# Two column chunks of a feed-forward tile computed side by side in two PSUM banks, in a two-block transformer kernel on one core

## Chip, cores and metric

The kernel runs on one core of a Trainium2 chip. The metric is the device time of one execution in microseconds (us). Before the change the median of three runs is 4473.61 us (4471.12 to 4476.59).

## What is computed

Two blocks in sequence work on 1024 tokens of width 1024 (and, in the first block, 256 context tokens). Each has two layers. The change touches only the feed forward of the second block, which runs once per layer:

```
def conv_ffn(h, w_up, conv_w, conv_b, w_down):
    up = h @ w_up                                  # 1024 -> 2 * 2816
    padded = jnp.pad(up, ((0, 0), (2, 0), (0, 0)))
    conv = conv_b + padded[:, 0:s_len] * conv_w[0]
    for j in range(1, 3):
        conv = conv + padded[:, j:j + s_len] * conv_w[j]
    gate, val = jnp.split(conv, 2, axis=-1)
    return (jax.nn.silu(gate) * val) @ w_down      # 2816 -> 1024
```

Everything is float32. The kernel gets that precision from three matmuls in a rounded format for each product: a value is split into a rounded part (hi) and the rest (lo), and w_hi\*hi + w_hi\*lo + w_lo\*hi is summed.

## The kernel before, in words

**Layout.** Activations lie with channels on the 128 partitions and the 1024 tokens along the free dimension. A weight tile is 128 output channels; it is an entry of the list SEQ with its number g, its count nk of 128-row contraction steps, and its column chunks. In the feed forward every tile has two chunks of 512 tokens (CH_LAT). The 2816 hidden channels are 22 pairs f of up tiles, tile 2f (gate) and tile 2f+1 (value), with nk = 8. The down projection is done in six groups of hidden channels, (0,4), (4,8), (8,12), (12,16), (16,19), (19,22), each with eight output tiles d of nk = 4 or 3. A group's down tiles stand behind the up tiles of f = 4, 8, 12, 16, 19 and 21 (the dictionary AFTER), so that a group's last activation has one f of time to be made.

**Chunks and banks.** All chunks of the program are numbered q in order, and chunk q is accumulated in PSUM bank q % 3 (psum_of). So a chunk can start when chunk q-3 has been taken out of its bank: PE (TensorE) waits for `acc_free{q % 3}` to reach q // 3, and when the last matmul of a chunk has finished it raises `acc_ready`.

**PE, lines 498 to 514 (project).** A tile waits for its split weights (`w_split`), then chunk after chunk: wait for the bank, then for each of the nk rows the three matmuls of lines 511, 512 and 513. A tile of nk = 8 has 2 x 24 matmuls of 512 columns. Lines 471 to 495 (row_tile, project_as_ready) take both chunks of a row in turn, three matmuls in each bank, because the rows become ready one at a time; the first up tile of a layer is done so. The feed forward's order on PE is lines 916 to 928.

**ACT (ScalarE), lines 1308 to 1322.** For each f in order: the four up chunks are copied out of PSUM (line 1178, in evacuate2), each as soon as it is ready; then ACT waits for the convolution of f on DVE (`ff_conv`) and applies Silu (line 1320), waits for the product (`ff_prod`) and writes g_hi (line 1322). Only then does it turn to the chunks of f+1:

```
for f in range(NF):
    n = NF * l + f
    up(f)
    act.wait_ge(sem["ff_conv"], n + 1)
    A(ff_c[0], ff_c[0], ACT.Silu).then_inc(sem["ff_gated"], 1)
    act.wait_ge(sem["ff_prod"], n + 1)
    A(g_hi[:, f % NG], ff_c[1], ACT.Copy).then_inc(sem["ff_hi"], 1)
```

**DVE (VectorE), lines 1745 to 1782.** For each f: it waits until all four chunks are copied (`ff_up_ready`), computes the convolution of the gate and the value tile (lines 1765, 1767, 1769, twice), waits for Silu, multiplies (1775), waits for g_hi, writes g_lo (1779) and raises `g_ready`. Where down tiles follow on PE, it adds their 16 chunks to the residual (line 1757) and frees their banks, one chunk between every two of those steps, the rest afterwards; for f = 21 all adds come at the end.

**POOL (GpSimd), lines 1795 to 1804.** Splits the weights of tile g into w_hi (1802) and w_lo (1803), once all chunks of tile g-2 are ready. SP (SyncE) loads the weights, two tiles ahead.

Of the kernel before, what the change touches and what calls it, by code (L numbers as in the profile page):

```python
# [19 lines left out]
P = 128  # L20
# [21 lines left out]
NG = 5  # L42
# [9 lines left out]
def stream():  # L52

    seq = []
    for l in range(2):
        for i, n in enumerate(IN1):
            seq.append(("in1", l, i, 8, CH_ALL if l == 0 or n in KV1 else CH_LAT))
        for d in range(DT):
            seq.append(("out1", l, d, 8, CH_ALL if l == 0 else CH_LAT))
    for l in range(2):  # L60
        for i, n in enumerate(IN2):
            seq.append(("in2", l, i, 8, CH_LAT))
        for d in range(DT):
            seq.append(("out2", l, d, 8, CH_LAT))
        for f in range(NF):
            seq.append(("up", l, 2 * f, 8, CH_LAT))
            seq.append(("up", l, 2 * f + 1, 8, CH_LAT))
            if f in AFTER:
                g = AFTER[f]
                for d in range(DT):  # L70
                    seq.append(("down", l, (g, d), GROUPS[g][1] - GROUPS[g][0], CH_LAT))
    return seq


SEQ = stream()
INDEX = {e[:3]: g for g, e in enumerate(SEQ)}
FIRST_CHUNK = np.cumsum([0] + [len(e[4]) for e in SEQ]).tolist()
# [66 lines left out]
def two_mixers(nc, xT, cT, w_mod, w_in1, w_out1, vec1, vec2, vec3, sinks, gla_up,  # L144
# [5 lines left out]
    def put(name, floats, dt=F32, where=None):  # L150
        offset = at[0] if where is None else where
        place[name] = offset
        if where is None:
            at[0] += (floats + -floats % 8) * 4
        assert offset + floats * 4 <= 229368, name
        return nc.alloc_sbuf_tensor_at(name, [P, floats], dt, offset=offset)

    raw = put("raw", 2 * 1024)
    w_hi = put("w_hi", 2 * 1024, F32R)
    w_lo = put("w_lo", 2 * 1024, F32R)  # L160
# [23 lines left out]
    h2_hi = h2_hi_[:, :].rearrange("p (j t) -> p j t", t=S)  # L184
    h2_lo = h2_lo_[:, :].rearrange("p (j t) -> p j t", t=S)
# [18 lines left out]
    def k(name):  # L204
        c, n = CONST_AT[name]
        if name in ("dec", "qdec", "kdec"):
            c -= NC1
            return cst2[:, c:c + n]
        if c > NC1:
            c -= 2048  # L210
        return cst[:, c:c + n]


    a = Area(wk1, 0, n1)
# [4 lines left out]
    a = Area(wk1, 0, n1)  # L219
# [5 lines left out]
    a = Area(wk1, 0, n1)  # L225
# [9 lines left out]
    a = Area(wk1, 0, n1)  # L235
# [7 lines left out]
    a = Area(gw, 0, 2 * DT * T)  # L243
# [16 lines left out]
    a = Area(wk2, 0, n2)  # L260
# [3 lines left out]
    a = Area(wk2, 0, n2)  # L264
# [9 lines left out]
    a = Area(wk2, 0, n2)  # L274
# [8 lines left out]
    g_hi = put("g_hi", NG * S, F32R, where=work2)[:, :].rearrange("p (f t) -> p f t", t=S)  # L283
    g_lo = put("g_lo", NG * S, F32R, where=work2 + NG * S * 4)[:, :].rearrange("p (f t) -> p f t", t=S)
    a = Area(wk2, 2 * NG * S, n2)
# [24 lines left out]
    sem = {n: nc.alloc_semaphore(n) for n in names}  # L310
# [40 lines left out]
    def psum_of(q):  # L351
        return psum[q % 3]


    with block:
# [111 lines left out]
        def _(pe):  # L467
            mm = nc.tensor.matmul
# [22 lines left out]
            def project_as_ready(g, hi, lo, ready, before):  # L491

                for kt in range(SEQ[g][3]):
                    row_tile(g, kt, hi, lo, ready, before)

            def project(g, hi, lo, f0=None, only=None):

                _, _, _, nk, chunks = SEQ[g]
                pe.wait_ge(sem["w_split"], g + 1)
                wh, wl = w_hi[:, (g % 2) * 1024:], w_lo[:, (g % 2) * 1024:]  # L500
                for ci, (t0, n) in enumerate(chunks):
                    if only is not None and ci != only:
                        continue
                    q = FIRST_CHUNK[g] + ci
                    if q >= 3:
                        pe.wait_ge(sem[f"acc_free{q % 3}"], q // 3)
                    o = psum_of(q)[:, 0:n]
                    for kt in range(nk):
                        ws = slice(kt * P, (kt + 1) * P)
                        at_ = kt if f0 is None else (f0 + kt) % NG  # L510
                        mm(o, wh[:, ws], hi[:, at_, t0:t0 + n], start=kt == 0, stop=False)  # L511
                        mm(o, wh[:, ws], lo[:, at_, t0:t0 + n], start=False, stop=False)  # L512
                        last = mm(o, wl[:, ws], hi[:, at_, t0:t0 + n], start=False, stop=kt == nk - 1)  # L513
                    last.then_inc(sem["acc_ready"], 1)

            def modulate(row, w):

                for kt in range(DT):
                    last = mm(row, csil[:, 2 * kt:2 * kt + 2], w[:, :, kt * P:(kt + 1) * P], start=kt == 0, stop=kt == DT - 1)
                last.then_inc(sem["wm_used"], 1)  # L520
# [9 lines left out]
            def add_square(n, j, chunks, sq):  # L530

                pe.wait_ge(sem["sq_ready"], 8 * n + j + 1)
                for ci, (t0, w) in enumerate(chunks):
                    last = mm(psum[3 + ci][:, 0:w], k("ones"), sq[j % 2][:, t0:t0 + w], start=j == 0, stop=j == 7)  # L534
                last.then_inc(sem["sq_used"], 1)
# [7 lines left out]
            for u in range(4):  # L543
                pe.wait_ge(sem[f"wm_in{u}"], 16)
                modulate(START_BANKS[u][0:2, :], gw[:, u * 4096:(u + 1) * 4096].rearrange("p (m c) -> p m c", c=D))
                if u:
                    turn_modulation(u - 1, 4, mod_row[:, (u - 1) * 512:u * 512], 4 * (u - 1))
            turn_modulation(3, 4, mod_row[:, 1536:2048], 12)
            for l in layers:
# [4 lines left out]
                chunks = CH_OUT[l]  # L554
                c0 = chunk_count(l)
                if l == 0:
# [9 lines left out]
                    a = len(LATE_MOD)  # L566
                    turn_modulation(3 + a, 2, mod_row[:, (a - 1) % 2 * 256:], 2 * (a - 1))
                project(proj_index(l, "bk"), h_hi, h_lo)
                for j in range(2):
                    pe.wait_ge(sem["conv_ready"], 2 * l + j + 1)  # L570
                    for ci, (t0, w) in enumerate(chunks):
                        last = mm(psum[3 + ci][:, 0:w], k("ones256"), cv_a[j][:, t0:t0 + w], start=j == 0, stop=j == 1)
                last.then_inc(sem["mean_ready"], 1)
                for j in range(2):
                    pe.wait_ge(sem["csq_ready"], 2 * l + j + 1)
                    for ci, (t0, w) in enumerate(chunks):
                        last = mm(psum[3 + ci][:, 0:w], k("ones256"), cv_sq[:, t0:t0 + w], start=j == 0, stop=j == 1)
# [16 lines left out]
                for t in range(NTT):  # L594
                    last = nc.tensor.transpose(psum[3 + t // 4][:, (t % 4) * P:(t % 4 + 1) * P], at_raw[:, t * P:(t + 1) * P], ident)
# [68 lines left out]
                for t in range(NTT):  # L664
                    mm(psum[3 + t // 2][:, (t % 2) * 256:(t % 2 + 1) * 256], gl_lr[:, t * P:(t + 1) * P], gl_up,
                       start=True, stop=True).then_inc(sem["z_ready"], 1)
# [90 lines left out]
                for n, t in enumerate(BORD):  # L757
                    gt = NTT * l + n
                    pe.wait_ge(sem["sb_ready"], gt + 1)
                    if outs or t < NBLK:  # L760
                        if n >= 2:
                            pe.wait_ge(sem["obb_added"], outputs(l, n) - 2)
                        for c in (1, 0):
                            for j in range(2):
                                last = mm(psum[5 + n % 2][:, j * P + c * 64:j * P + (c + 1) * 64],
                                          gl_s[(2 * n + 1 - c) % 6][:, j * P:(j + 1) * P],
                                          gl_qd[:, 1, t * P + c * 64:t * P + (c + 1) * 64],
                                          start=(c, j) == (1, 0), stop=c == 0, skip_group_check=True)
# [4 lines left out]
                for j in range(2):  # L773
                    for ci, (t0, w) in enumerate(chunks):
                        b, o = [(3, 0), (4, 0), (5, 0)][ci] if j == 0 else [(6, 0), (7, 0), (5, 256)][ci]
                        last = mm(psum[b][:, o:o + w], k("ones64"), gl_sq[:, j * T + t0:j * T + t0 + w], start=True, stop=True)
# [10 lines left out]
            for l in layers:  # L787
# [6 lines left out]
                for t in range(NBLK):  # L794
                    for j in range(2):
                        o = (t % 2) * 256 + j * P
                        last = nc.tensor.transpose(psum[3 + t // 2][:, o:o + P], sg_v[j][:, t * P:(t + 1) * P], ident)
# [3 lines left out]
                for j in range(2):  # L801
                    for n in range(NBLK):
                        for h in (2 * j, 2 * j + 1):
                            last = mm(psum[3 + 2 * j + n // 4][:, (n % 4) * P:(n % 4 + 1) * P], sg_vz[:, n, h, :],
                                      sg_ws[:, h * P:(h + 1) * P], start=h % 2 == 0, stop=h % 2 == 1)
# [3 lines left out]
                for j in range(2):  # L809
# [5 lines left out]
                    for ci in range(2):  # L815
                        last = mm(psum[3 + ci][:, :], po_w[:, j * P:(j + 1) * P], po_p[j][:, ci * 512:(ci + 1) * 512], start=True, stop=True)
# [55 lines left out]
                for j in range(4):  # L872
# [19 lines left out]
                    for t in range(NBLK):  # L892
                        last = mm(psum[5 + t // 4][:, (t % 4) * P:(t % 4 + 1) * P], re_kd[:, t * P:(t + 1) * P],
                                  re_v[:, t * P:(t + 1) * P], start=True, stop=True)
# [21 lines left out]
                for f in range(NF):  # L916
                    if f == 0:
                        project_as_ready(INDEX[("up", l, 0)], h2_hi, h2_lo, "h_ready", nh)
                    else:
                        project(INDEX[("up", l, 2 * f)], h2_hi, h2_lo)  # L920
                    project(INDEX[("up", l, 2 * f + 1)], h2_hi, h2_lo)
                    if f in AFTER:
                        g = AFTER[f]
                        f0, f1 = GROUPS[g]
                        pe.wait_ge(sem["g_ready"], NF * l + f1)
                        for d in range(DT):
                            project(INDEX[("down", l, (g, d))], g_hi, g_lo, f0)
                            if f == NF - 1 and d:
                                add_square(5 + 2 * l, d - 1, CH_LAT, f_sq)
                add_square(5 + 2 * l, DT - 1, CH_LAT, f_sq)  # L930
# [1057 lines left out]
```

## Time and profile before

| | |
|---|---|
| median of three runs | 4473.61 us |
| span of the profiled execution, first to last instruction | 4469.6 us |
| PE busy | 4037.1 us, 90% |
| DVE, ACT, POOL busy | 43%, 24%, 25% |
| mean granted TensorE clock | 0.960 of full speed |
| matmuls of lines 511 to 513, all parts | 12552 |
| feed forward, layer 0 and layer 1 of the second block | about 2386 to 3150 us and 3680 to 4450 us |

The profiled execution has no time of its own beside its span; the span lies 4.0 us below the median of the runs, which is what lies around it and the spread between runs. Busy shares are averages over parts with different limits. Matmuls overlap in the pipeline: a row's duration (0.39 us) is longer than the distance to the next start (0.23 us), so a rate is read from starts. "Idle before" is the time in which the engine had nothing in flight, and the releaser is what ended it.

### The profile page before, as it was taken

To read this page: it belongs to the slowest core of one execution; us is meant where nothing else is said; L and a number is where in the kernel's file an instruction comes from. 1 tells how busy PE (TensorE), PEld (TensorE's weight loads), DVE (VectorE), ACT (ScalarE), POOL (GpSimd) and SP (SyncE) were. 2 spreads that over 40 slices of the span, in tenths; PEclk is the share of its full clock that TensorE was granted. 3 is DMA by queue.
4 is the path that set the end of the run, shared out by engine and by line. 5 is a ranking of instruction groups with operands and counts; after the bars stand their busy time and mean duration, and the time that the engine had idled before them with its cause. 6 is when DMAs were issued, how large, how long until landed. Compare 5 with 4: busy or idle time off the path is not lost.

```text
span 4469.6 us, 46828 instructions
## 1 busy us (share of the span) xinstructions
PE 4037.1 (90%) x18692; PEld 3153.4 (71%) x18692; DVE 1938.5 (43%) x2630; ACT 1066.3 (24%) x1934; POOL 1105.8 (25%) x764
## 2 busy tenths in 40 slices
PE   6979999798399998899989999998999799999997
PEld 3657778686277776578766888886677567888885
DVE  2655651815656445332324454444333325444543
ACT  3014542202145421312312111111222312111112
POOL 0021002222110121133312333333233123333331
PEclk9989999999699998999989999999999899999998
DMA  4310000022000001211111111111210021111111
GB/s 158 133 61 20 10 12 15 27 69 84 10 20 10 21 5 52 94 48 34 38 48 47 48 43 43 50 46 39 89 38 34 24 71 36 52 50 48 48 48 52
DMA packets 60857, 209.22 MB, mean 47 GB/s; under 512 B 6752, under 2 KB 11872, under 8 KB 59488
## 3 DMA queue, kind: packets, MB, share of 16 engines
q1 hardware_dynamic: 60640, 206.22, 13.5%
q8 instruction: 149, 2.44, 0.2%
q14 instruction: 68, 0.56, 0.0%
HBM read 189.42 MB, written 16.78 MB: 46 GB/s over the span
## 4 chain that ended last, share of the span: by engine, by line
PE 78%; DVE 16%; ACT 3%; issue 2%; DMA 1%; POOL 0%; SPq 0%; DVEq 0%; ACTq 0%; POOLq 0%
PE bank L511 21%; PE bank L512 20%; PE bank L513 20%; DVE wk L1414 4%; PE bank L534 2%; PE bank L630 2%; DVE wk L1359 2%; PE bank L616 1%; DVE h_lo L1348 1%; DVE gw L1538 1%; DVE gw L1549 1%; PE bank L607 1%; PE bank L605 1%; DVE wk L1471 1%; PE bank L485 1%
## 5 line engine op out<-in xcount | busy, mean ns | idle before, releaser
L511 PE MATMUL bank<-h_hi,w_hi 128*128 128x512 f32 (+1 forms) x3480 | 1370.3, 394 | 16.8 <-POOLq L1804 9.3
L512 PE MATMUL bank<-h_lo,w_hi 128*128 128x512 f32 (+1 forms) x3480 | 1344.6, 386 | 0.0
L513 PE MATMUL bank<-h_hi,w_lo 128*128 128x512 f32 (+1 forms) x3480 | 1344.4, 386 | 0.0
L1802 POOL CAST w_hi<-raw 128x1024 fp32r<-128x1024 f32 (+2 forms) x306 | 302.7, 989 | 2565.2 <-PE bank L513 1954.5
L511 PEld LDWEIGHTS bank<-h_hi,w_hi 128*128 128x128 f32 x3480 | 657.3, 189 | 173.3 <-issue 17.6
L512 PEld LDWEIGHTS bank<-h_lo,w_hi 128*128 128x128 f32 x3480 | 657.1, 189 | 152.4 <-issue 12.2
L513 PEld LDWEIGHTS bank<-h_hi,w_lo 128*128 128x128 f32 x3480 | 656.5, 189 | 143.2
L1803 POOL TENSOR_TENSOR w_lo<-raw,w_hi 128x1024 fp32r<-128x1024 f32 (+2 forms) x306 | 638.3, 2086 | 24.5
L511 PE MATMUL bank<-g_hi,w_hi 128*128 128x512 f32 x704 | 284.5, 404 | 26.6 <-DVEq L1780 26.6
L1765 DVE TENSOR_SCALAR wk<-wk,v 128x1024 f32<-128x1024 f32 x88 | 86.7, 986 | 478.3 <-ACTq L1314 475.5
L1178 ACT ACTIVATE wk<-bank 128x512 f32<-128x512 f32 x192 | 114.4, 596 | 742.8 <-PE bank L513 733.1
L512 PE MATMUL bank<-g_lo,w_hi 128*128 128x512 f32 x704 | 279.3, 397 | 0.0
L513 PE MATMUL bank<-g_hi,w_lo 128*128 128x512 f32 x704 | 279.1, 396 | 0.0
L1757 DVE TENSOR_TENSOR x<-bank,x 128x512 f32<-128x512 f32 x192 | 132.8, 692 | 243.1 <-PE bank L513 238.5
L485 PE MATMUL bank<-h_hi,w_hi 128*128 128x512 f32 x176 | 86.8, 493 | 133.6 <-DVE h_lo L1348 71.6
L1414 DVE SCALAR_TENSOR_TENSOR wk<-wk,v 128x1024 f32<-128x1024 f32 (+1 forms) x180 | 191.1, 1090 | 4.3
L1767 DVE SCALAR_TENSOR_TENSOR wk<-wk,v 128x1024 f32<-128x1024 f32 x88 | 186.2, 2116 | 5.3
L511 PEld LDWEIGHTS bank<-g_hi,w_hi 128*128 128x128 f32 x704 | 133.3, 189 | 61.6 <-DVEq L1780 27.5
L630 PE MATMUL bank<-wk 128*128 128x128 f32 x1280 | 166.5, 276 | 0.0
L1320 ACT ACTIVATE wk<-wk 128x1024 f32<-128x1024 f32 x44 | 46.7, 1061 | 465.3 <-DVEq L1772 465.3
L512 PEld LDWEIGHTS bank<-g_lo,w_hi 128*128 128x128 f32 x704 | 133.3, 189 | 33.9 <-issue 2.9
L485 PEld LDWEIGHTS bank<-h_hi,w_hi 128*128 128x128 f32 x176 | 40.5, 230 | 163.9 <-issue 64.8
(247 smaller groups left out, 4714.9 us busy)
## 6 DMA issues: line engine op xcount, KB each, us to landing
raw<-w_in SPq DMA_DIRECT2D x90, 512.0 KB, 3.5
raw<-w_ffn SPq DMA_DIRECT2D x88, 512.0 KB, 3.5
x<-w_mod SPq DMA_DIRECT2D x16, 1024.0 KB, 4.8
raw<-w_out SPq DMA_DIRECT2D x32, 512.0 KB, 4.4
raw<-w_down SPq DMA_DIRECT2D x64, 256.0 KB, 2.6
residual<-x SPq DMA_DIRECT2D x3, 4096.0 KB, 12.0
wk<-residual SPq DMA_DIRECT2D x24, 512.0 KB, 3.5
gw<-w_mod SPq DMA_DIRECT2D x4, 2048.0 KB, 23.4
```

Of the source, the lines that this page charges most:

```text
L485: mm(o, wh[:, ws], hi[:, kt, t0:t0 + n], start=kt == 0, stop=False)
L511: mm(o, wh[:, ws], hi[:, at_, t0:t0 + n], start=kt == 0, stop=False)
L512: mm(o, wh[:, ws], lo[:, at_, t0:t0 + n], start=False, stop=False)
L513: last = mm(o, wl[:, ws], hi[:, at_, t0:t0 + n], start=False, stop=kt == nk - 1)
L534: last = mm(psum[3 + ci][:, 0:w], k("ones"), sq[j % 2][:, t0:t0 + w], start=j == 0, stop=j == 7)
L630: last = mm(out_bank(i)[:, 0:P], at_vz[:, kt, g, :], at_pt[i % 2][:, c * P:(c + 1) * P], start=g == 0 and c == 0, stop=g == 1 and c == len ...
L1178: link(A(dst[:, t0:t0 + w], psum_of(q)[:, 0:w], func, scale=scale))
L1414: ins = V.scalar_tensor_tensor(dst, src, vl("conv_w", 31 * j + i), dst, ALU.mult, ALU.add)
L1757: link(V.tensor_tensor(x2[:, d, t0:t0 + w], psum_of(q)[:, 0:w], x2[:, d, t0:t0 + w], ALU.add))
L1767: link(V.scalar_tensor_tensor(c, u[:, 1:S + 1], w2("conv_w", 44 + wi), c, ALU.mult, ALU.add))
L1802: link(G.tensor_copy(w_hi[:, sl], raw[:, sl]))
L1803: link(G.tensor_tensor(w_lo[:, sl], raw[:, sl], w_hi[:, sl].bitcast(F32), ALU.subtract))
```

## The change

In the feed forward, project is replaced by project_side_by_side for every tile but the first up tile of a layer. The new function works in nk + 2 steps. In a step it takes row `step` of chunk 0 and row `step - 2` of chunk 1, and each of the three terms is issued for chunk 0 and then for chunk 1, so that consecutive matmuls go to two banks in turn. In the first two steps there is only chunk 0, in the last two only chunk 1. PE waits for the bank of chunk 0 at the tile's start and for that of chunk 1 before the third step.

```
@@ -512,6 +512,30 @@
+            def project_side_by_side(g, hi, lo, f0=None):
+
+                _, _, _, nk, chunks = SEQ[g]
+                pe.wait_ge(sem["w_split"], g + 1)
+                wh, wl = w_hi[:, (g % 2) * 1024:], w_lo[:, (g % 2) * 1024:]
+                (t0, n), (t1, _) = chunks
+                q0, q1 = FIRST_CHUNK[g], FIRST_CHUNK[g] + 1
+                o0, o1 = psum_of(q0)[:, 0:n], psum_of(q1)[:, 0:n]
+                pe.wait_ge(sem[f"acc_free{q0 % 3}"], q0 // 3)
+                lead = 2
+                for step in range(nk + lead):
+                    k0, k1 = step, step - lead
+                    if k1 == 0:
+                        pe.wait_ge(sem[f"acc_free{q1 % 3}"], q1 // 3)
+                    for term in range(3):
+                        w, v = (wl if term == 2 else wh), (lo if term == 1 else hi)
+                        for kt, o, t, q in ((k0, o0, t0, q0), (k1, o1, t1, q1)):
+                            if 0 <= kt < nk:
+                                a = kt if f0 is None else (f0 + kt) % NG
+                                last = mm(o, w[:, kt * P:(kt + 1) * P], v[:, a, t:t + n], start=kt == 0 and term == 0,
+                                          stop=kt == nk - 1 and term == 2)
+                                if kt == nk - 1 and term == 2:
+                                    last.then_inc(sem["acc_ready"], 1)
@@ -917,14 +941,14 @@
                     if f == 0:
                         project_as_ready(INDEX[("up", l, 0)], h2_hi, h2_lo, "h_ready", nh)
                     else:
-                        project(INDEX[("up", l, 2 * f)], h2_hi, h2_lo)
-                    project(INDEX[("up", l, 2 * f + 1)], h2_hi, h2_lo)
+                        project_side_by_side(INDEX[("up", l, 2 * f)], h2_hi, h2_lo)
+                    project_side_by_side(INDEX[("up", l, 2 * f + 1)], h2_hi, h2_lo)
...
                         for d in range(DT):
-                            project(INDEX[("down", l, (g, d))], g_hi, g_lo, f0)
+                            project_side_by_side(INDEX[("down", l, (g, d))], g_hi, g_lo, f0)
```

## Rows read from the trace of the kernel before

**Rows 1.** The page: the clock line, and the chain that ended last by engine.
```profile
PEclk9989999999699998999989999999999899999998
...
PE 78%; DVE 16%; ACT 3%; issue 2%; DMA 1%; POOL 0%; SPq 0%; DVEq 0%; ACTq 0%; POOLq 0%
```
**Rows 2.** A group by line, page: count, busy, mean ns, idle before, releaser.
```profile
L511 PE MATMUL bank<-g_hi,w_hi 128*128 128x512 f32 x704 | 284.5, 404 | 26.6 <-DVEq L1780 26.6
```
**Rows 3.** Busy time by stretch: us, PE, PEld, DVE, ACT, POOL, PEclk, DMA, GB/s.
```profile
2416.00:3020.00 604.00, 604.00 (x2590) 485.84 (x2589) 289.72 (x216) 84.84 (x115) 205.70 (x141) 1.00 0.14 46
3700.00:4340.00 640.00, 640.00 (x2756) 518.86 (x2755) 310.24 (x237) 88.75 (x119) 220.32 (x155) 1.00 0.15 47
```
**Rows 4.** Timeline of ACT, one f: start, duration, line [idle before <-releaser].
```profile
2616.55 0.60 ACT L1178 ACTIVATE wk<-bank 128x512 f32<-128x512 f32 x1 [5.00 <-PE bank L513]
...
2628.89 1.06 ACT L1322 ACTIVATE g_hi<-wk 128x1024 fp32r<-128x1024 f32 x1 [1.35 <-DVEq L1776]
2629.86 1.29 ACT L1178 ACTIVATE wk<-bank 128x512 f32<-128x512 f32 x2
2633.35 0.60 ACT L1178 ACTIVATE wk<-bank 128x512 f32<-128x512 f32 x1 [2.20 <-PE bank L513]
```
**Rows 5.** Timeline of PE: chunk ends (L513) and starts (L511) within one f.
```profile
2616.12 0.39 PE L513 MATMUL bank<-h_hi,w_lo 128*128 128x512 f32 x1
2616.35 0.40 PE L511 MATMUL bank<-h_hi,w_hi 128*128 128x512 f32 x1
...
2627.55 0.40 PE L511 MATMUL bank<-h_hi,w_hi 128*128 128x512 f32 x1
...
2632.92 0.39 PE L513 MATMUL bank<-h_hi,w_lo 128*128 128x512 f32 x1
2633.15 0.40 PE L511 MATMUL bank<-h_hi,w_hi 128*128 128x512 f32 x1
```
**Rows 6.** Timeline: a matmul that waited for a bank, earlier in the program.
```profile
105.67 0.60 ACT L998 ACTIVATE wk<-bank 128x512 f32<-128x512 f32 x1
106.45 0.47 PE L511 MATMUL bank<-h_hi,w_hi 128*128 128x512 f32 x1 [1.10 <-ACTq L999]
106.76 0.39 PE L512 MATMUL bank<-h_lo,w_hi 128*128 128x512 f32 x1
```
**Rows 7.** Timeline of DVE beside down tiles of nk = 4.
```profile
2644.62 0.69 DVE L1757 TENSOR_TENSOR x<-bank,x 128x512 f32<-128x512 f32 x1 [0.67 <-PE bank L513]
2645.45 2.26 DVE L1769 SCALAR_TENSOR_TENSOR wk<-wk,v 128x1024 f32<-128x1024 f32 x1
```
**Rows 8.** Timeline of PE: one row of a tile taken in two banks.
```profile
1041.35 0.39 PE L486 MATMUL bank<-h_lo,w_hi 128*128 128x512 f32 x1
1041.58 0.40 PE L487 MATMUL bank<-h_hi,w_lo 128*128 128x512 f32 x1
1041.81 0.40 PE L485 MATMUL bank<-h_hi,w_hi 128*128 128x512 f32 x1
1042.06 0.40 PE L486 MATMUL bank<-h_lo,w_hi 128*128 128x512 f32 x1
```
**Rows 9.** Timeline of PE: 256 columns; then 512 columns at a lower clock.
```profile
308.08 0.28 PE L511 MATMUL bank<-h_hi,w_hi 128*128 128x256 f32 x1
308.20 0.28 PE L512 MATMUL bank<-h_lo,w_hi 128*128 128x256 f32 x1
...
2387.42 0.63 PE L485 MATMUL bank<-h_hi,w_hi 128*128 128x512 f32 x1
2387.85 0.63 PE L486 MATMUL bank<-h_lo,w_hi 128*128 128x512 f32 x1
```
**Rows 10.** Busy time by stretch, columns as above, around short idle times of PE.
```profile
1040.50:1054.50 14.00, 8.54 (x32) 5.76 (x33) 12.17 (x22) 5.91 (x9) 0.07 (x1) 1.00 0.00 0
...
312.00:316.00 4.00, 2.38 (x6) 1.93 (x7) 0.00 (x0) 1.51 (x6) 1.63 (x1) 0.64 0.31 70
...
2386.50:2391.00 4.50, 4.50 (x12) 3.41 (x11) 4.43 (x5) 2.11 (x2) 0.00 (x0) 0.50 0.00 0
```

## The prediction

> **What bounds the kernel now.** I read the page first. TensorE is granted the full clock nearly everywhere, and the chain that ended last is 78% PE [rows 1]; in the feed forward it is PE alone, so I looked there for anything that PE waits for. The groups by line show no wait on a bank: the 704 first matmuls of the down tiles have 26.6 us of idle time, all for g_lo of the last f (13.3 us per layer) [rows 2]. The busy time by stretch then says that PE has no idle time at all over 604 and 640 us [rows 3]. The reader should see two things there: the stage's time is the number of matmuls times their distance, and 604/2590 is 0.2332 us, 640/2756 is 0.2322 us. So the change can act in two ways only: on that distance, or by making PE wait where it now does not.
>
> The second needs the order on ACT. ACT copies the last chunk of an f at 2616.55, then waits for DVE twice, ends g_hi at 2628.89 + 1.06 = 2629.95, and only then takes the first chunk of the next f out of its bank, two chunks in one row from 2629.86 [rows 4]. That chunk had been complete since about 2622, 5.6 us after the f began. It hurts nobody now: the bank is wanted by the fourth chunk, and that starts at 2633.15 [rows 5].
>
> **The change, part by part.** I call the four chunks of an up pair a0 to a3.
>
> *Matmuls, loads, semaphores.* The number of matmuls, of weight loads and of signals stays the same; a0 of a tile is ready after 41 of 48 matmuls instead of after 24, a1 at the tile's end as before. POOL's split waits for whole tiles, so its start, SP's loads and the collisions of POOL with DVE stay where they are relative to the tile's end. No term.
>
> *The wait for the bank of a3.* Bank q % 3 makes a3 wait for a0. Before, a3 starts 24 matmuls into the second tile. Now PE asks for its bank after 6 matmuls, in front of the third step, and all that PE has left of the tile is queued behind that wait. The second tile starts at 2627.55 [rows 5]; 6 matmuls of 0.2333 later is 2628.95. The copy of a0 starts at 2629.86 and takes 0.60 like the single ones [rows 4], so it ends at 2630.46. Where PE has waited for such a copy, its matmul started 0.18 us after the copy's end (105.67 + 0.60 = 106.27, start 106.45), and the next came 0.31 later instead of 0.23 [rows 6]. PE resumes at 2630.64: 1.69 us of wait, 0.08 for the slower start, 1.77 in all. ACT's chain hangs on the end of the previous f and not on a0, so nothing in this change shortens it.
>
> *How often.* It happens where the f before has no down tiles behind it: with them, DVE and ACT are through with that f long before a0 is ready. Of f = 0 to 21, f = 0 and those behind 4, 8, 12, 16 and 19 are free of it, which leaves 16 per layer, 32 in all. In layer 1 the same reading shifts by a few hundredths, since the matmuls are 0.2322 apart; I don't carry that. 32 x 1.77 = **+56.6 us**. Bounds: 32 x 1.4 = 45 if the copy were handed over at once and the last matmuls before the wait overlapped it, 32 x 2.1 = 67 if the hand-over cost twice what it does in rows 6.
>
> *The other banks.* a1 wants the bank that held a2 of the f before. Now a2 is complete 7 matmuls before its tile's end and a1 begins 6 matmuls into the next: 13 x 0.233 = 3.0 us for a copy of 0.60 plus hand-over. ACT waits for exactly that copy then. Nothing. The down tiles have the same 3.0 us for their first chunk, where they had two chunks, 5.6 or 4.2 us; their cover is DVE, whose add takes 0.69 but can stand behind a step of up to 2.26 us [rows 7]. The last matmul ends and hands over in some 0.4 us (started 2632.92, copied from 2633.35 [rows 4, 5]), so 0.43 + 0.69 + 0.18 = 1.3 leaves about 2.0 us for DVE. Setting DVE's steps against the new completion times (4.0, 5.6, 9.6, 11.2 us and so on for nk = 4, 2.6, 4.2, 6.8, 8.4 for nk = 3) I find the adds in time; in the worst phase one is late by 0.3 us, and 12 groups x 4 such adds x 0.3 = 14 us is the upper bound. I take 0. At f = 21 all adds come afterwards, one per chunk, and have room.
>
> *The distance between matmuls.* The tiles done side by side are 86 of nk = 8, 64 of nk = 4 and 32 of nk = 3. In the two first and two last steps one chunk runs alone (12 matmuls), so 36, 12 and 6 matmuls of a tile alternate: 3096 + 768 + 192 = 4056 of 6240. Does a change of bank help? In a tile taken row by row at full clock the distances are 0.23 in one bank, 0.23 over the change of bank (1041.58 to 1041.81) and 0.25 behind it [rows 8]; the change from a3 to the next a0 is 0.23 too, 2616.12 to 2616.35 [rows 5]. And what a matmul takes beyond one column per cycle goes with its columns: 256 columns are 0.12 apart, half of 0.233, while at half clock 512 columns are 0.43 apart, 512 cycles of 1.2 GHz and nothing more [rows 9, 10]. A cost of reopening the same bank would be a constant per matmul. I take **0**. Bounds: the best is one column per cycle at 2.4 GHz, 0.2133 us, 20 ns less; the worst is 0.01 more, half of what rows 8 show behind a change.
>
> What 20 ns would bring is less than 4056 x 20 = 81 us. In each of the 32 waiting f the gain of the first tile (36 x 20 ns = 0.72 us) only makes PE arrive earlier at the same wait: 32 x 0.72 = 23 us are swallowed, 58 us remain. The worst side is 4056 x 0.01 = 41 us, less what the wait swallows, 29.
>
> The Trainium skill (TensorE: Matmul & The Clock Gate, Back-to-back issue gap) gives a warm matmul of N columns as N / 2.4 plus 2.5 ns, 215.8 ns for 512. The trace differs: 0.2322 to 0.2333 us. By that rule as the goal of the alternation the sum would be about 4473.6 + 57 - 2904 x 17 ns = 4481 us.
>
> **Sum.** 4469.6 + 56.6 = 4526.2 us of span for the profiled execution; the median of the runs is 4.0 above that span, so **4530 us**, 1.3% slower. About 0.2% (9 us) is what a measurement of this kernel can tell from no change.
>
> **The rivals.**
>
> *A. The alternation brings the matmuls down to a column per cycle.* Against it: rows 5, 8 and 9. For it: one change of bank in 24 or in 3 matmuls is not a change at every one. 4530 - 58 = 4472 us, no difference. Chance 0.06. The two parts would then cancel.
>
> *B. Matmuls into different banks overlap, and the kernel is faster.* The place is the same, the 2904 alternating matmuls (4056 less 32 x 36) that are not swallowed. It decides from 66 / 2904 = 23 ns of gain on, a distance below 0.2107 us, which is under the column per cycle; so two matmuls would have to stream at once. If the bank were all the limit, the distance could halve: 2904 x 0.1167 = 339 us, 4191 us. Nothing in the rows speaks for it; the half clock's 0.43 is just the columns. Chance 0.03.
>
> *C. The new waits make the clock fall.* PE is idle for some 1.5 us every 24 us. For it: around idle times of that length the clock was 0.64 in one stretch; against it: it stayed 1.00 over four waits of 1.64 us in 14 us, with PE busy in 8.54 of them [rows 10], and here PE is busy before and behind. If it fell each time for six matmuls (at 312 to 316), 6 x 0.2 = 1.2 us, 32 x 1.2 = 38 us: 4568 us. Chance 0.08. The same page of the Trainium skill (A second HAM failure mode) says that cycling through PSUM banks lets PE idle briefly between groups, so that the clock goes up and down; by it C would be likelier than I make it. The trace before cycles through three banks and shows 1.00 in both stretches [rows 3].
>
> *D. The bank's waits are as forecast, and DVE's adds or a slower change of bank come on top.* 4530 + 14 + 29 = 4573 at the most, 4545 in the middle. Chance 0.11.
>
> *E. The wait is covered after all,* because the copy of a0 comes earlier than I read it. The order on ACT is written out and nothing moves it, so only if my reading of which bank is wrong: 4474 us. Chance 0.02.
>
> **How the numbers follow.** The forecast has 0.70, within 4518 to 4542 by the bounds of the wait. With D up to 4552 and a part of a smaller gain on the other side I come to the range 4512 to 4556, about 8 in 10; C's top and A, B, E stay outside. Faster by over 0.2%: B, 0.03. Within 0.2%: A (where its gain is nearly whole) and E, 0.06. Slower: the rest, 0.91.
>
> **What the changed profile would show.** Idle time of PE with the copy of line 1178 on ACT as releaser, 32 times, about 1.5 us each and 50 us in all (the rest is drain and slower start), none for f behind down tiles; the distance from one f to the next in such a pair 24.2 us instead of 22.4; the distance between alternating matmuls 0.232 to 0.233; DVE's adds without PE waiting for them; the clock 1.00 in both stretches. I am wrong if the distance falls below 0.23, if the waits are fewer or for another engine, or if the clock drops behind them.

## The result, and the profile after

| | before | after |
|---|---|---|
| median of the runs | 4475.07 us (4471.12 to 4476.59, 4 runs) | 4529.37 us (4527.12 to 4530.09, 4 runs) |
| span of the profiled execution | 4469.6 us | 4525.3 us |
| ratio to before | | 1.0123, 95% interval 1.0109 to 1.0138 |

The median before counts one run more than the one given ahead of the prediction (4473.61 us). The changed kernel is 1.2% slower, 54 us by the medians and 55.7 us by the spans; the prediction was 4530 us.

The page of the changed kernel has these lines against [rows 1, 2]. Line 535 is the one matmul line of the new function; ACT's copy of an up chunk, line 1178 before, is now line 1202, and ACT's signal for a free bank is line 1203.

```profile
PEclk9989999899699999999999999999999899999998
PE 68%; DVE 23%; ACT 5%; issue 2%; DMA 1%; POOL 0%; DVEq 0%; SPq 0%; ACTq 0%; POOLq 0%
L535 PE MATMUL bank<-h_hi,w_hi 128*128 128x512 f32 x1376 | 463.0, 397 | 46.5 <-ACTq L1203 46.5
...
L535 PE MATMUL bank<-g_hi,w_hi 128*128 128x512 f32 x704 | 258.0, 403 | 26.6 <-DVEq L1804 26.6
```

The clock line is as before but for a digit in three slices, and the mean is 0.959 of full speed where it was 0.960. In the chain that ended last PE has 68% where it had 78%; DVE has 23% where it had 16%, and ACT 5% where it had 3%. In the up tiles there are 46.5 us of idle time that did not exist, all for one releaser; the down tiles have what they had, 26.6 us for g_lo of the last f, and nothing for DVE's adds. (All matmuls of the new function have line 535, so the page tells them apart by their operands. Where two consecutive ones have the same operands, a timeline prints one row, "x2", whose time runs from the start of the first to the end of the second.)

The waits view of the changed kernel: engine, line and what it waited for, total us, times, longest.

```profile
PE bank L535 <- ACTq L1203: 46.5, 32, 1.5
```

32 waits, as counted in the prediction. The stretch of busy time that answers to the first of [rows 3]:

```profile
2416.00:3020.00 604.00, 583.64 (x2495) 468.50 (x2494) 275.51 (x208) 80.76 (x109) 204.34 (x136) 1.00 0.15 45
```

PE was busy for all of the 604 us before and misses 20.4 us now, with 95 matmuls fewer in the same time; the clock is 1.00 in both. In the second stretch of [rows 3] the changed kernel has 30.1 us of idle time and a clock of 0.99. The low clock there lies before 3714 us, where the feed forward of that layer has not yet come to its first wait (3750.62):

```profile
3700.00:3714.00 14.00, 6.70 (x17) 4.94 (x17) 9.97 (x9) 7.83 (x9) 0.00 (x0) 0.63 0.13 39
3714.00:4340.00 626.00, 603.20 (x2574) 482.96 (x2573) 285.20 (x220) 86.74 (x116) 207.35 (x138) 1.00 0.15 44
```

One wait, in the timeline of ACT (start, duration, line, idle time before):

```profile
2602.99 0.60 ACT L1202 ACTIVATE wk<-bank 128x512 f32<-128x512 f32 x1 [1.03 <-PE bank L535]
2612.93 1.06 ACT L1344 ACTIVATE wk<-wk 128x1024 f32<-128x1024 f32 x1 [9.33 <-DVEq L1796]
2615.34 1.06 ACT L1346 ACTIVATE g_hi<-wk 128x1024 fp32r<-128x1024 f32 x1 [1.35 <-DVEq L1800]
2616.30 1.30 ACT L1202 ACTIVATE wk<-bank 128x512 f32<-128x512 f32 x2
2625.44 0.60 ACT L1202 ACTIVATE wk<-bank 128x512 f32<-128x512 f32 x1 [7.84 <-PE bank L535]
2627.07 0.60 ACT L1202 ACTIVATE wk<-bank 128x512 f32<-128x512 f32 x1 [1.03 <-PE bank L535]
```

and in that of PE:

```profile
2614.87 0.39 PE L535 MATMUL bank<-h_lo,w_hi 128*128 128x512 f32 x1
2615.10 0.40 PE L535 MATMUL bank<-h_hi,w_lo 128*128 128x512 f32 x1
2616.97 0.72 PE L535 MATMUL bank<-h_hi,w_hi 128*128 128x512 f32 x2 [1.48 <-ACTq L1203]
2617.53 0.63 PE L535 MATMUL bank<-h_lo,w_hi 128*128 128x512 f32 x2
2618.00 0.63 PE L535 MATMUL bank<-h_hi,w_lo 128*128 128x512 f32 x2
```

ACT's chain from the last chunk of an f to the copy of the next f's first chunk is what it was: 2602.99 to 2616.30 is 13.31 us, and 2616.55 to 2629.86 was 13.31 us [rows 4]. PE has issued 6 matmuls of the second tile, would issue the next at 2615.33, and starts at 2616.97: 1.64 us late. The first pair then takes 0.56 us instead of 0.47. Together 1.73 us. This is one of the longer waits: its idle time is 1.48 us, and the mean of the 32 is 46.5 / 32 = 1.45. From one f's last copy to the next it is 2627.07 - 2602.99 = 24.08 us, against 22.40 before in this layer (96 matmuls of 0.2333 us).

### The profile page after: what moved, and what is told of

It is laid out like the page before. It is cut to its first block, busy times and chain, and to the rows that moved or that the text cites. A ratio compares the mean times of both kernels' runs of the same rounds, so it can differ in the third digit from the quotient of the medians.

```text
span 4525.3 us, 46828 instructions
## 1 busy us (share of the span) xinstructions
PE 4046.4 (89%) x18692; PEld 3154.1 (70%) x18692; DVE 1931.1 (43%) x2630; ACT 1066.1 (24%) x1934; POOL 1115.9 (25%) x764
## 4 chain that ended last, share of the span: by engine, by line
PE 68%; DVE 23%; ACT 5%; issue 2%; DMA 1%; POOL 0%; DVEq 0%; SPq 0%; ACTq 0%; POOLq 0%
PE bank L535 23%; PE bank L511 10%; PE bank L513 9%; PE bank L512 9%; DVE wk L1438 4%; DVE wk L1791 3%; PE bank L558 2%; PE bank L654 2%; DVE wk L1793 2%; DVE wk L1383 2%; DVE wk L1789 1%; PE bank L640 1%; DVE h_lo L1372 1%; DVE gw L1573 1%; DVE wk L1799 1%
## 5 line engine op out<-in xcount | busy, mean ns | idle before, releaser
L511 PE MATMUL bank<-h_hi,w_hi 128*128 128x512 f32 (+1 forms) x2104 | 827.2, 393 | 16.7 <-POOLq L1828 9.1
L512 PE MATMUL bank<-h_lo,w_hi 128*128 128x512 f32 (+1 forms) x2104 | 801.4, 381 | 0.0
L513 PE MATMUL bank<-h_hi,w_lo 128*128 128x512 f32 (+1 forms) x2104 | 801.1, 381 | 0.0
L535 PE MATMUL bank<-h_hi,w_hi 128*128 128x512 f32 x1376 | 463.0, 397 | 46.5 <-ACTq L1203 46.5
L511 PEld LDWEIGHTS bank<-h_hi,w_hi 128*128 128x128 f32 x2104 | 398.6, 189 | 111.5 <-issue 17.7
L535 PE MATMUL bank<-h_hi,w_lo 128*128 128x512 f32 x1376 | 459.6, 395 | 0.0
L535 PE MATMUL bank<-h_lo,w_hi 128*128 128x512 f32 x1376 | 459.5, 395 | 0.0
L513 PEld LDWEIGHTS bank<-h_hi,w_lo 128*128 128x128 f32 x2104 | 397.7, 189 | 81.4
L535 PEld LDWEIGHTS bank<-h_hi,w_hi 128*128 128x128 f32 x1376 | 256.5, 188 | 118.5 <-ACTq L1203 60.4
L535 PEld LDWEIGHTS bank<-h_hi,w_lo 128*128 128x128 f32 x1376 | 259.0, 188 | 61.1
L535 PEld LDWEIGHTS bank<-h_lo,w_hi 128*128 128x128 f32 x1376 | 259.0, 188 | 61.1
L535 PE MATMUL bank<-g_hi,w_hi 128*128 128x512 f32 x704 | 258.0, 403 | 26.6 <-DVEq L1804 26.6
L535 PE MATMUL bank<-g_hi,w_lo 128*128 128x512 f32 x704 | 252.9, 396 | 0.0
L535 PE MATMUL bank<-g_lo,w_hi 128*128 128x512 f32 x704 | 252.6, 396 | 0.0
L485 PE MATMUL bank<-h_hi,w_hi 128*128 128x512 f32 x176 | 86.5, 491 | 133.7 <-DVE h_lo L1372 72.4
```

Of the source, the lines that this page charges most:

```text
L535: last = mm(o, w[:, kt * P:(kt + 1) * P], v[:, a, t:t + n], start=kt == 0 and term == 0, stop=kt == nk - 1 and term == 2)
```

## The experiments

Three explanations were set against each other. **Mine:** all of the loss is the wait for the bank of the first up chunk, and the alternation itself does nothing. **Rival 1:** the alternation (or each change of bank) costs time on PE. **Rival 2:** DVE's adds come late beside the down tiles. A further one (rival 3): the alternation gains something that the wait hides. The kernel before was run beside each group; its medians there were 4472.75 us (first four), 4473.89 us (the leads) and 4474.23 us (the last). Each edit but the last is made to the changed kernel.

### Only the up tiles

```
-                            project_side_by_side(INDEX[("down", l, (g, d))], g_hi, g_lo, f0)
+                            project(INDEX[("down", l, (g, d))], g_hi, g_lo, f0)
```

> Side by side in the up tiles alone, the down tiles as before the change. My theory (all of the loss is the wait of the fourth up chunk for the bank of the first, which ACT copies only after g_hi): the whole loss stays, 32 waits of 1.4 to 1.5 us, 4529 us. Rival 1 (the alternation of banks itself costs time on PE, everywhere): about two thirds of the loss would belong to the up tiles by their count of alternating matmuls (3096 of 4056), so 4516 us. Rival 2 (the adds of DVE beside the down tiles come late): 4475 plus what is left, below 4520 us.

Measured: 4530.12 us, ratio 1.0128 (1.0112 to 1.0145). The whole loss is in the up tiles. The group of their first matmuls:

```profile
L535 PE MATMUL bank<-h_hi,w_hi 128*128 128x512 f32 x1376 | 462.9, 397 | 46.8 <-ACTq L1203 46.8
```

### Only the down tiles

```
-                        project_side_by_side(INDEX[("up", l, 2 * f)], h2_hi, h2_lo)
-                    project_side_by_side(INDEX[("up", l, 2 * f + 1)], h2_hi, h2_lo)
+                        project(INDEX[("up", l, 2 * f)], h2_hi, h2_lo)
+                    project(INDEX[("up", l, 2 * f + 1)], h2_hi, h2_lo)
```

> Side by side in the down tiles alone. My theory: DVE's adds are in time for the bank although its first chunk is ready 3.0 us ahead of the need instead of 5.6 or 4.2 us: 4475 us, no PE idle time with DVE's line 1757 as releaser, at most 14 us more. Rival 1 (alternation costs): 960 of 4056 alternating matmuls, 4488 us. Rival 2 (late adds): 4480 us or more, with waits of PE for DVE in the trace.

Measured: 4473.72 us, ratio 1.0001 (0.9992 to 1.0011), and no wait of PE for DVE's adds in the trace. Nothing, so rival 2 is out, and rival 1 too as far as the 960 alternating matmuls of the down tiles go.

### The bank changes at every third matmul

```
-                    for term in range(3):
-                        w, v = (wl if term == 2 else wh), (lo if term == 1 else hi)
-                        for kt, o, t, q in ((k0, o0, t0, q0), (k1, o1, t1, q1)):
+                    for kt, o, t, q in ((k0, o0, t0, q0), (k1, o1, t1, q1)):
+                        for term in range(3):
+                            w, v = (wl if term == 2 else wh), (lo if term == 1 else hi)
                             if 0 <= kt < nk:
```

> As changed, but within a step the three matmuls of chunk 0 come first and then the three of chunk 1: the bank changes at every third matmul instead of at every one, and the wait stands at the same place. My theory: the alternation does nothing, 4529 us, the same 32 waits. Rival 1 (each change of bank costs): two thirds of it gone, 4493 us. Rival 3 (each change of bank gains, and the wait costs more than I priced): 4529 plus up to 50 us.

Measured: 4527.17 us, ratio 1.0122 (1.0106 to 1.0137), 32 waits and 46.7 us of idle time. The changed kernel had 1.0123 with the bank changing at every matmul. Rival 1 had 4493 us for this order. Whether matmuls go to the banks in turn or by threes makes no difference that can be seen.

### ACT copies the first chunk before g_hi

In the loop over f on ACT; the rest of up(f) then skips that chunk.

```
                     A(ff_c[0], ff_c[0], ACT.Silu).then_inc(sem["ff_gated"], 1)
+                    if f not in AFTER:
+                        take_up(f + 1, 0, 0)
                     act.wait_ge(sem["ff_prod"], n + 1)
```

> As changed, and ACT copies the first chunk of the next f between Silu and g_hi, where no down tiles follow the f. My theory: the copy then ends about 11.8 us after the f before, handed over at 12.0, and PE asks for the bank at 12.4: no wait, g_hi is not late since ACT waited 1.35 us for DVE's product there anyway; 4475 us, the kernel before. Rival 1 (alternation costs): still well above, 4500 us or more. Rival 3 (alternation gains, hidden by the wait): below 4475, down to 4394 us for a column per cycle.

Measured: 4475.99 us, ratio 1.0008 (0.9998 to 1.0017). PE's order is that of the changed kernel, and the waits are gone. The timeline of ACT in this kernel (line 1335 is the copy, 1352 Silu, 1356 g_hi):

```profile
2597.42 0.60 ACT L1335 ACTIVATE wk<-bank 128x512 f32<-128x512 f32 x1 [1.03 <-PE bank L535]
2607.35 1.06 ACT L1352 ACTIVATE wk<-wk 128x1024 f32<-128x1024 f32 x1 [9.33 <-DVEq L1806]
2608.32 0.58 ACT L1335 ACTIVATE wk<-bank 128x512 f32<-128x512 f32 x1
2609.76 1.06 ACT L1356 ACTIVATE g_hi<-wk 128x1024 fp32r<-128x1024 f32 x1 [0.87 <-DVEq L1810]
```

and PE's group of the same matmuls:

```profile
L535 PE MATMUL bank<-h_hi,w_hi 128*128 128x512 f32 x1376 | 459.2, 395 | 0.0
```

The copy starts 10.9 us behind the last copy of the f before instead of 13.3, and sits in ACT's idle time ahead of g_hi. With all 4056 matmuls still alternating the time is that of the kernel before: rival 1 and rival 3 both fall here. The upper end of the interval leaves 7.6 us, under 2 ns for each alternating matmul. An alternation worth 20 ns a matmul would have given 4394 us.

### The lead of the first chunk: 1, 3, 4 and 5 rows

```
-                lead = 2
+                lead = 1
```

and likewise 3, 4 and 5. Each row of lead puts PE's question for the bank 3 matmuls, 0.70 us, later.

> As changed with a lead of one row: PE asks for the bank after 3 matmuls instead of 6. My theory: each of the 32 waits grows by 3 matmuls, 0.70 us, 32 x (1.74 + 0.70) = 78 us, 4551 us from them alone; beside the down tiles DVE's cover shrinks from 2.0 to 0.6 us, so adds come late there for the first time (10 groups x up to 4 adds x 0.7 us = 28 us at the most), 4565 us in the middle. Rival (the loss goes with the matmuls that alternate, 42 of 48 instead of 36): 4473 + 56 x 42/36 = 4538 us.

> A lead of three rows. My theory: each wait is 0.70 us shorter, 32 x 1.04 = 33 us, 4506 us. Rival (the loss goes with the alternating matmuls, 30 of 48): 4520 us.

> A lead of four rows. My theory: each wait is 1.40 us shorter than as changed, 32 x 0.34 = 11 us, 4484 us, and hardly any of it as idle time of PE. Rival (24 of 48 alternate): 4510 us.

> A lead of five rows: PE asks for the bank 15 matmuls into the tile, 3.5 us, and it is free 3.1 us into it. My theory: no wait, 4473 us, although 18 of 48 matmuls of an up tile still alternate. Rival (the loss goes with them): 4501 us.

| lead | median us | ratio to before | above 4473.9 | my theory | rival 1 | idle of L535 for the bank |
|---|---|---|---|---|---|---|
| 1 | 4573.69 | 1.0219 (1.0204 to 1.0235) | 99.8 | 78 + up to 28 | 65 | 68.8 |
| 2, the change | 4529.37 | 1.0123 (1.0109 to 1.0138) | 54.3 beside its own before | 56 | 56 | 46.5 |
| 3 | 4506.08 | 1.0065 (1.0048 to 1.0082) | 32.2 | 33 | 47 | 24.6 |
| 4 | 4482.04 | 1.0016 (1.0007 to 1.0026) | 8.2 | 11 | 37 | 2.2, no releaser named |
| 5 | 4475.44 | 1.0000 (0.9990 to 1.0009) | 1.6 | 0 | 28 | none |

From lead 2 to lead 4 the loss falls by 22 and 24 us for a row, against 32 waits x 0.70 us = 22.4, and it ends at lead 5, where PE comes after the copy. The columns "my theory" and "rival 1" are what each gives above the kernel before. The idle times, one line of each kernel for leads 1 and 3:

```profile
L535 PE MATMUL bank<-h_hi,w_hi 128*128 128x512 f32 x1376 | 456.6, 403 | 68.8 <-ACTq L1203 68.8
```

```profile
L535 PE MATMUL bank<-h_hi,w_hi 128*128 128x512 f32 x1376 | 476.9, 397 | 24.6 <-ACTq L1203 24.6
```

Lead 1 has an extra that I had put in the wrong place. I expected late adds beside the down tiles, up to 28 us. The groups show 0.4 us for those in all:

```profile
L535 PE MATMUL bank<-g_hi,w_hi 128*128 128x512 f32 x704 | 243.9, 405 | 27.0 <-DVEq L1804 26.6 <-DVEq L1782 0.4
```

But the matmuls of the up tiles in the first line above have a mean of 403 ns instead of 397. The waits of four consecutive f in the timeline of PE, and the busy time by stretch behind the first and the third wait (the clock stands behind the five busy times):

```profile
2428.56 0.80 PE L535 MATMUL bank<-h_hi,w_hi 128*128 128x512 f32 x2 [2.18 <-ACTq L1203]
2429.16 1.05 PE L535 MATMUL bank<-h_lo,w_hi 128*128 128x512 f32 x2
2430.01 1.05 PE L535 MATMUL bank<-h_hi,w_lo 128*128 128x512 f32 x2
...
2454.89 0.73 PE L535 MATMUL bank<-h_hi,w_hi 128*128 128x512 f32 x2 [2.12 <-ACTq L1203]
...
2481.20 0.73 PE L535 MATMUL bank<-h_hi,w_hi 128*128 128x512 f32 x2 [2.17 <-ACTq L1203]
...
2505.93 0.73 PE L535 MATMUL bank<-h_hi,w_hi 128*128 128x512 f32 x2 [2.17 <-ACTq L1203]
```

```profile
2429.00:2433.00 4.00, 4.00 (x12) 3.11 (x11) 2.26 (x1) 0.18 (x1) 1.18 (x1) 0.57 0.43 113
...
2481.00:2485.00 4.00, 3.80 (x16) 3.12 (x17) 2.90 (x1) 0.70 (x2) 1.82 (x1) 1.00 0.22 63
```

Behind the first wait the clock is 0.57 over 4 us, that is 1.2 GHz for most of it, and a pair of matmuls takes 0.85 us from start to start instead of 0.47; behind the third it stays at 2.4 GHz. So the distances from wait to wait are 26.33, 26.31 and 24.73 us. In the granted clock of this execution 13 of the 32 waits are followed by such a fall; in the executions of the changed kernel, of the up tiles alone and of the grouped order, with 32 waits of up to 1.5 us each, none is. 13 x 1.6 = 21 us, and 78 + 21 = 99, about the measured loss of 99.8.

### Rows that are ready, done ahead of the wait

This one starts from the kernel before and is about its only idle time in the stage, 13.3 us per layer for g_lo of f = 21 [rows 2]. PE does the rows of f = 19 and 20 of the first three chunks of the last group before that wait:

```
+                        if f == NF - 1:
+                            pe.wait_ge(sem["g_ready"], NF * l + f1 - 1)
+                            last_rows(l, g, ((0, 0), (0, 1), (1, 0)), (0, 1))
                         pe.wait_ge(sem["g_ready"], NF * l + f1)
...
+                            if f == NF - 1 and d < 2:
+                                last_rows(l, g, ((0, 0), (0, 1)) if d == 0 else ((1, 0),), (2,))
+                                if d:
+                                    project(INDEX[("down", l, (g, d))], g_hi, g_lo, f0, only=1)
+                            else:
+                                project(INDEX[("down", l, (g, d))], g_hi, g_lo, f0)
```

last_rows issues, for each of the chunks (d, ci), the three matmuls of the given rows, and waits for weights and bank where it does row 0.

> The kernel before, and in the last group of down tiles PE does the rows of f = 19 and 20 of the first three chunks (18 matmuls) before it waits for g_lo of f = 21, where it was idle for 13.3 us in each layer. My theory: 18 x 0.233 = 4.2 us per layer of work moved into idle time, 2 x 4.2 = 8.4 us, 4464 us from 4473; the matmuls behind the wait run as slowly as now. Rival (the shorter idle time also spares part of the low clock, 8 matmuls at 0.43 instead of 0.23, 1.6 us per layer): 4461 us. Rival (the wait is not the limit there, since the adds and squares at the end follow DVE and ACT): 4473 us.

Measured: 4462.73 us, ratio 0.9973 (0.9964 to 0.9983), faster than the kernel before by its interval. So the rival that the wait is no limit there (4473 us) is out. The wait is now in line 529 of this kernel:

```profile
L529 PE MATMUL bank<-g_hi,w_hi 128*128 128x512 f32 x18 | 8.8, 491 | 18.3 <-DVEq L1807 18.3
```

26.6 - 18.3 = 8.3 us of idle time are filled, the 8.4 us of the expectation. The medians differ by 11.5 us, and the interval reaches from 8 to 16 us, so the rest may be spread. The profiled executions show where more can come from: from the first to the last down matmul layer 1 takes 645.8 us (3795.80 to 4441.61) instead of 649.9 (3797.54 to 4447.45), which is the 4.1 us filled, and layer 0 takes 645.7 (2509.19 to 3154.91) instead of 652.6 (2504.35 to 3156.90). The 2.7 us by which layer 0 gains more come from the faster pace described in the last section, which the down-only kernel has in layer 0 too, so it is not the edit's doing.

The rival that the clock is spared (1.6 us per layer) finds little in the rows. In layer 1, 7 matmuls behind the wait stand 0.43 us apart in this kernel, from 4401.08 on,

```profile
4400.48 0.80 PE L529 MATMUL bank<-g_hi,w_hi 128*128 128x512 f32 x1 [9.18 <-DVEq L1807]
4401.08 0.63 PE L530 MATMUL bank<-g_lo,w_hi 128*128 128x512 f32 x1
...
4404.06 0.46 PE L531 MATMUL bank<-g_hi,w_lo 128*128 128x512 f32 x1
4404.37 0.39 PE L511 MATMUL bank<-g_hi,w_hi 128*128 128x512 f32 x1
```

and 6 in the kernel before; in layer 0 it is 6 here and 8 before. Together that is one matmul fewer, 0.2 us and not 3.2.

## Why the prediction was right, point by point

- **The wait and its place.** Predicted: 32 waits of a3 for the bank of a0, because ACT copies a0 only behind g_hi. Found: 32, with that releaser. Shown by edits, not only argued: the order on ACT alone takes them away (1.0008), the lead moves them by 3 matmuls at a time, and the up tiles alone have all of them.
- **Its price.** Predicted 1.69 + 0.08 = 1.77 us; found 1.64 + 0.09 = 1.73 in the wait shown. The first of the two copies in that row ends at 2616.88, so PE started 0.10 us after the copy's end and not 0.18 as in [rows 6]. With the shorter waits counted the 32 come to about 55 us, against 55.7 us by the spans. The visible idle time was 46.5 us where I had written 50, from the same 0.1 us per wait.
- **The gain of the first tile is swallowed by the wait.** Not tested by itself, since there was no gain.
- **Alternating banks brings nothing.** Right. The reading behind it was that the excess over a column per cycle goes with the columns and that a change of bank has the same distance [rows 5, 8, 9]. The grouped order and the moved copy show it for all 4056 matmuls. So rival A (4472 us) and rival B (4191 us) fall. The goal that I took from the Trainium skill (TensorE: Matmul & The Clock Gate, Back-to-back issue gap), 215.8 ns for 512 columns, was not approached by any order tried here: the distance stayed at 0.232 to 0.233 us.
- **DVE's adds are in time.** Right at lead 2: side by side in the down tiles alone gives 1.0001. Even at lead 1 only 0.4 us of waits appeared. My bound of 14 us for this term was far too wide; it also counted all 12 groups of the two layers, though it says itself that the adds of f = 21 come afterwards and have room, which leaves 10.
- **Rival C, the clock.** Wrong for the change, where the clock is 1.00 behind the waits of 1.5 us; right at lead 1, where 13 of 32 waits of 2.2 us were followed by a fall at 1.6 us each (the rival had 1.2). The prediction had nothing that set a limit between 1.5 and 2.2 us: its two examples had almost the same idle time and opposite outcomes [rows 10]. That the change stayed on the harmless side was therefore in part luck. The Trainium skill (TensorE: Matmul & The Clock Gate, A second HAM failure mode: psum-queue depth-cycling) ties a clock that goes up and down to the short idle times of PE that come with cycling through PSUM banks. Here the banks were cycled in every kernel, and in the up tiles the clock fell behind a wait only in the one with idle times of 2.2 us; cycling by itself did not do it.
- **Sum.** 4530 predicted, 4529.37 measured, and this closeness is luck. Two terms were too dear: the wait by at least 0.04 us (1.3 us in all), and the matmuls of layer 0, which ran faster than in the kernel before (below, about 3 us). Something outside the sum made up for both: from the last down matmul of layer 0 to the first of layer 1 the changed kernel took 650.4 us (3182.31 to 3832.68) and the kernel before 640.6 (3156.90 to 3797.54), and the four waits in between explain 6.9 of these 9.7 us. The kernel with side by side in the down tiles alone, which has none of these waits, took 643.9 us there, so the rest belongs to what one execution differs from another.

## What to carry to other kernels

Before an order of matmuls is changed, follow each bank it touches to the engine that frees it, and ask when that engine gets to it: here the consumer's written-out order fixed the moment, 13.3 us behind the copy of the last chunk of an f, and PE's question for it was moved 4.2 us forward past it. Working on two accumulations at once takes two banks for most of the tile, so with three banks in rotation it gives away the cover that doing them one after another had. Work that needs nothing late (rows that are ready, a copy that fits in an engine's idle time) is what can be moved; the order in which banks are written was worth nothing by itself here.

## What had not been expected of the hardware

- **The clock behind a short idle time.** PE's idle time of 1.5 us once in 24 us left the granted clock at 2.4 GHz behind all 32 waits, and so it did in the two other kernels with lead 2 and these waits; idle times of 2.2 us were followed by 1.2 GHz in 13 cases of 32. What sets the 13 apart from the other 19 was not found. From lead 2 to lead 1 a wait longer by 0.7 us so cost 1.4 us more on the average ((99.8 - 54.3) / 32).
- **Two paces of the same matmul at the same clock.** Consecutive matmuls of 512 columns are 0.2333 us apart in layer 0 of the kernel before and 0.2322 in layer 1 [rows 3], at a granted clock of 1.00 in both. In the changed kernel it is 0.232 in layer 0 as well: the adds of every second down chunk there are 5.57 us apart, 24 matmuls, where before it was 5.60.

```profile
2682.95 0.69 DVE L1781 TENSOR_TENSOR x<-bank,x 128x512 f32<-128x512 f32 x1 [3.27 <-PE bank L535]
...
2688.53 0.69 DVE L1781 TENSOR_TENSOR x<-bank,x 128x512 f32<-128x512 f32 x1 [3.25 <-PE bank L535]
...
2694.10 0.69 DVE L1781 TENSOR_TENSOR x<-bank,x 128x512 f32<-128x512 f32 x1 [3.25 <-PE bank L535]
```

  It is not the alternation: the down-only kernel has 5.58 in layer 0 and 5.60 in layer 1, the kernel before the other way round, and the last experiment, with nearly the order of before, has the faster pace in both (604 us for 2601 matmuls and 640 us for 2755 in the stretches of [rows 3]). For 3120 matmuls a layer it is 3 us, about what one execution differs from another. What sets it stays open.
